# Second mixer of a fused transformer kernel: another order of masks, exponentials, weight splits and norms on three engines

## The reference, cut to what matters

```
h = rms_norm_2(x, attn_norm);  proj = h @ w_in                  # 1024 -> 5444 columns
aq, ak, av, iq, ik, iw, bq, bk, bv, gates = split_cols(proj)
aq, ak, bq, bk = rope(head-wise rms_norm of each); iq = rope(iq); ik = rope(rms_norm(ik))
score = sum_h iw[h] * relu(iq[h] . ik / 8);  keep the 64 best causal keys of each query
ya = softmax(aq . ak / 8 over the kept keys) @ av               # sparse, 8 heads
lam = exp(sum(dl0*dl1)) - exp(sum(dl2*dl3)) + lam_init
yb = (softmax(bq0 . bk0) - lam * softmax(bq1 . bk1)) @ bv       # differential, 4 heads
yb = rms_norm(yb, b_subln) * (1 - lam_init)
x = x + (sigmoid(g_a) * (ya @ w_up_a) + sigmoid(g_b) * (yb @ w_up_b)) @ w_out
```

## Time and profile before

| what | value |
|---|---|
| runs of the kernel before | 1838.51, 1839.82, 1843.36 us; median 1839.82 us |
| the profiled execution | 1841.48 us, its span 1839.8 us |
| PE busy | 1794.3 us, 98% of the span |
| DVE busy | 1122.3 us, 61% |
| ACT busy | 936.7 us, 51% |
| POOL busy | 195.0 us, 11% |
| mean granted TensorE clock | 0.998 of full |
| mixer 2 of layer 0, of layer 1 | tile 0 at 1050.3 us, at 1442.3 us of the span |

### The profile page before, as it was taken

One profiled execution on the slowest core, in us unless ns is written; L12 is line 12 of the kernel. 1 busy time (PEld: TensorE's weight loads), 2 busy tenths in 40 slices (PEclk: granted clock), 3 DMA queues, 4 the chain that ended last, 5 costly groups with the idle time before them and its releaser, 6 DMA issues.

```text
span 1839.8 us, 23640 instructions
## 1 busy us (share of the span) xinstructions
PE 1794.3 (98%) x8740; PEld 1459.0 (79%) x8740; DVE 1122.3 (61%) x1649; ACT 936.7 (51%) x1266; POOL 195.0 (11%) x226
## 2 busy tenths in 40 slices
PE   7999999999999999999999999999999999999999
PEld 6888887788888888877888876778888777788887
DVE  5555676655555555777555489765554688765553
ACT  5444475544454444666444476655444656745441
POOL 0000020000000000200000095100001383000000
PEclk9999999999999999999999999999999999999999
DMA  8556462465556564543555464445555544345551
GB/s 254 184 191 222 139 184 93 151 197 191 196 157 189 190 218 143 181 130 123 186 192 196 160 206 142 156 138 175 187 194 190 203 145 155 130 147 181 186 207 64
DMA packets 221017, 316.21 MB, mean 172 GB/s; under 512 B 14056, under 2 KB 162176, under 8 KB 220672
## 3 DMA queue, kind: packets, MB, share of 16 engines
q1 hardware_dynamic: 220928, 315.03, 52.5%
HBM read 313.94 MB, written 1.05 MB: 171 GB/s over the span
## 4 chain that ended last, share of the span: by engine, by line
PE 81%; DVE 8%; issue 3%; ACT 3%; DVEq 2%; POOL 1%; DMA 1%; SPq 1%; POOLq 0%; ACTq 0%
PE ps L1829 25%; PE ps L1831 24%; PE ps L1830 24%; DVE w_lo L1145 2%; PE ps L1938 2%; ACT w_hi L679 1%; PE ps L1839 1%; PE ps L2034 1%; PE ps L2022 1%; PE ps L2010 1%; PE ps L1973 1%; DVE score L1604 1%; DVE att L1362 1%; DVEq L1607 1%; PE ps L2314 1%
## 5 line engine op out<-in xcount | busy, mean ns | idle before, releaser
L1145 DVE TENSOR_TENSOR w_lo<-raw,w_hi 128x2048 fp32r<-128x2048 f32 (+1 forms) x297 | 671.1, 2281 | 242.3 <-ACT w_hi L679 241.0
L1829 PE MATMUL ps<-w_hi,aT_hi 128*128 128x512 f32 (+2 forms) x1728 | 690.3, 399 | 12.9 <-DVE w_lo L1298 4.8
L1831 PE MATMUL ps<-w_hi,aT_lo 128*128 128x512 f32 (+2 forms) x1728 | 671.3, 388 | 0.0
L1830 PE MATMUL ps<-w_lo,aT_hi 128*128 128x512 f32 (+2 forms) x1728 | 669.4, 387 | 0.0
L679 ACT ACTIVATE w_hi<-raw 128x2048 fp32r<-128x2048 f32 (+1 forms) x297 | 554.7, 1899 | 182.4 <-PE ps L1831 178.8
L1829 PEld LDWEIGHTS ps<-w_hi,aT_hi 128*128 128x128 f32 x1728 | 325.8, 189 | 90.4 <-issue 15.2
L1831 PEld LDWEIGHTS ps<-w_hi,aT_lo 128*128 128x128 f32 x1728 | 325.4, 188 | 68.4
L1830 PEld LDWEIGHTS ps<-w_lo,aT_hi 128*128 128x128 f32 x1728 | 326.4, 189 | 59.6
L729 ACT ACTIVATE att<-ps,rstd 128x256 f32<-128x256 f32 x132 | 55.6, 472 | 377.9 <-PE ps L1831 377.8
L1219 DVE SCALAR_TENSOR_TENSOR att<-ps,rstd,att 128x256 f32<-128x256 f32 x132 | 57.8, 479 | 287.3 <-ACT att L729 287.3
L1829 PE MATMUL ps<-w_hi,gT_hi 128*128 128x512 f32 x528 | 207.1, 392 | 0.0
(11 more groups left out here) (265 smaller groups left out, 1398.0 us busy)
## 6 DMA issues: line engine op xcount, KB each, us to landing
raw<-in_w_in SPq DMA_DIRECT2D x120, 512.0 KB, 4.5
raw<-in_w_ffn_gate SPq DMA_DIRECT2D x88, 512.0 KB, 4.1
raw<-in_w_ffn_up SPq DMA_DIRECT2D x88, 512.0 KB, 5.1
raw<-in_w_ffn_down SPq DMA_DIRECT2D x88, 512.0 KB, 4.4
raw<-in_w_ffn_in SPq DMA_DIRECT2D x88, 512.0 KB, 4.9
raw<-in_w_ffn_out SPq DMA_DIRECT2D x44, 512.0 KB, 4.6
raw<-in_w_out SPq DMA_DIRECT2D x32, 512.0 KB, 4.7
raw<-in_w_ck SPq DMA_DIRECT2D x8, 512.0 KB, 4.2
```

The lines of the kernel that those rows point to most:

```text
L1145: V.tensor_tensor(o, a, h, ALU.subtract).then_inc(units_split, 1)
L1829: M(o, ah, wh, start=start, stop=False)
L1830: M(o, ah, wl, start=False, stop=False)
L1831: return M(o, al, wh, start=False, stop=stop)
```

## The change

Nothing is computed otherwise, except one added operation (below). Instructions trade places in the hand-written queues:

- **ACT, each feed-forward:** one Sqrt of a scratch column after the last `keep`, so that the Sqrt table is loaded there.
- **Start of mixer 2:** ACT splits unit 2 before it stages the second half (layer 0, as layer 1 did), and unit 3 after `evac(0)` in both layers. DVE in layer 1 takes `norm` before unit 3.
- **lam:** ACT's two Exp and DVE's three operations go from behind the first head norm to just ahead of `exps(0)` and `masked(0)`.
- **Turned keys:** `item(0)`, `item(1)`, `item(4)`, `item(5)` go ahead of head squares, sums or roots.
- **DVE:** `masked(0)`, `probs(0)` go ahead of the split of unit 12; `masked(0)` also ahead of one round of `best`; `probs(1)`, `masked(2)`, `masked(3)`, `probs(3)`, `masked(4)`, `probs(4)`, `probs(5)`, `probs(6)` ahead of a split or a gate; `up_a(1, ...)` ahead of the split of unit P2_OUT + 2.
- **ACT:** `exps(1)`, `exps(4)`, `exps(7)` ahead of a split, units 15 and 17 later; the first sigmoid from ahead of `probs_turned(6)` to behind `probs_turned(7)`.
- **PE:** six places at which turned keys or index scores are made are set one or two places later.
- **Mixer 1, DVE:** `probs(10)` ahead of `masked(11)`.

```diff
@@ ACT, ffn
                 keep(FT - 1, FT - 1)
+                act.wait_ge(consts_ready, 1)
+                nc.scalar.drain()
+                nc.scalar.activation(ms[:, 0:1], ident[:, 0:1], ACT.Sqrt)
@@ ACT, mixer 2
                 evac(0)
-                if l == 0:
-                    split(st, 3)
+                split(st, 3)
                 head_squares(0)
                 win_split(2, 0)
                 head_roots(0)
-                act.wait_ge(lam_sums, l + 1)
-                nc.scalar.activation(lam[:, 0:2], lam[:, 0:2], ACT.Exp).then_inc(lam_exp, 1)
                 win_split(2, 1)
...
                 evac(1)
+                item(0)
                 head_squares(1)
                 win_split(3, 1)
                 head_roots(1)
-                item(0)
...
                 win_split(5, 1)
+                item(4)
                 head_roots(3)
-                item(4)
                 win_split(6, 0)
+                act.wait_ge(lam_sums, l + 1)
+                nc.scalar.activation(lam[:, 0:2], lam[:, 0:2], ACT.Exp).then_inc(lam_exp, 1)
                 exps(0)
                 evac(4)
                 win_split(6, 1)
                 probs_turned(0)
+                exps(1)
                 split(st, P2_WIN + 14)
-                exps(1)
...
                 probs_turned(3)
+                exps(4)
                 split(st, P2_WIN + 19)
-                exps(4)
...
                 split(st, P2_UP)
-                act.wait_ge(tile_done, W + 9)
-                gate(GATES2 + DM)
                 probs_turned(6)
+                exps(7)
                 split(st, P2_UP + 1)
-                exps(7)
                 diff_hi()
                 split(st, P2_UP + 2)
                 probs_turned(7)
+                act.wait_ge(tile_done, W + 9)
+                gate(GATES2 + DM)
@@ DVE, mixer 1
+                probs(10)
                 masked(11)
-                probs(10)
@@ DVE, mixer 2
                 win_split(3, 0)
+                item(1)
                 head_sums(1)
                 win_split(3, 1)
                 head_scales(1)
-                item(1)
...
                 head_sums(3)
+                item(5)
                 win_split(5, 1)
                 head_scales(3)
                 best(1)
-                item(5)
-                best(1)
-                win_split(6, 0)
+                dve.wait_ge(lam_exp, l + 1)
+                V.tensor_tensor(lam[:, 2:3], lam[:, 1:2], lam[:, 0:1], ALU.subtract)
+                V.drain()
+                V.tensor_tensor(lam[:, 2:3], lam[:, 2:3], par2[:, 704:705], ALU.subtract)
                 masked(0)
                 best(1)
                 probs(0)
+                win_split(6, 0)
                 win_split(6, 1)
                 masked(1)
                 best(1)
+                probs(1)
                 split(st, P2_WIN + 14)
-                probs(1)
                 head_sums(4)
-                best(1)
-                split(st, P2_WIN + 15)
                 masked(2)
+                head_scales(4)
                 item(7)
-                head_scales(4)
                 best(1)
                 probs(2)
-                split(st, P2_WIN + 16)
+                split(st, P2_WIN + 15)
+                masked(3)
+                best(2)
+                probs(3)
                 best(1)
...
+                masked(4)
                 gate(7, 0)
-                masked(4)
+                probs(4)
                 dve.wait_ge(tile_done, W + 7)
                 gate(7, 1)
+                split(st, P2_WIN + 18)
+                probs_turned(4)
                 split(st, P2_WIN + 19)
-                probs(4)
-                probs_turned(4)
                 masked(5)
...
                 up_b(1)
-                split(st, P2_OUT + 2)
                 up_a(1, 0)
                 up_a(1, 1)
                 stage(B + 6, parts=((0, 1), (1, 1)), first=2, banks=STAGE_BANKS_UP)
+                split(st, P2_OUT + 2)
@@ PE, beside_bk: turn((0, 1)) at 6 -> 8, index_scores(0) at 13 -> 14
@@ PE, beside_aq: index_scores(2) at 1 -> 2, turn((2, 3)) at 6 -> 8
@@ PE, beside_bv: turn((4, 5)) at 9 -> 10, pair_qk(0) at 13 -> 14
```

More of the change, by code:

```diff
@@ L937, in _ @@
                     square_scaled(0)
+                    split(st, 2)
                     stage(B, GAIN_ATTN, PARTS[2:], first=2)
-                    split(st, 2)
                     square(6, 1, junk, 2)
@@ L944, in _ @@
                 else:
-                    turned_in(st, B, GAIN_ATTN + l * KC, l * 2 + 7, P2_WIN)
+                    stage(B, GAIN_ATTN + l * KC, PARTS[:2])
+                    square(l * 2 + 7, 0)
+                    split(st, 2)
+                    stage(B, GAIN_ATTN + l * KC, PARTS[2:], first=2)
+                    square(l * 2 + 7, 1)
+                    squared()
                     root(N)
@@ L1089, in _ @@
                 probs_turned(2)
-                split(st, P2_WIN + 17)
                 exps(3)
@@ L1093, in _ @@
                 item(8)
+                split(st, P2_WIN + 17)
                 split(st, P2_WIN + 18)
                 probs_turned(3)
+                exps(4)
                 split(st, P2_WIN + 19)
-                exps(4)
                 diff_out(3)
@@ L1550, in _ @@
                 else:
-                    turned_in(st, B, GAIN_ATTN + l * KC, P2_WIN)
+                    split(st, 2)
+                    stage(B, GAIN_ATTN + l * KC, PARTS[2:], first=2)
                     norm(N)
+                    split(st, 3)
                 dve.wait_ge(params2_loaded, (l + 1) * 128)
@@ L1702, in _ @@
                 head_scales(0)
-                dve.wait_ge(lam_exp, l + 1)
-                V.tensor_tensor(lam[:, 2:3], lam[:, 1:2], lam[:, 0:1], ALU.subtract)
-                V.drain()
-                V.tensor_tensor(lam[:, 2:3], lam[:, 2:3], par2[:, 704:705], ALU.subtract)
                 win_split(2, 1)
                 win_split(3, 0)
+                item(1)
                 head_sums(1)
@@ L1753, in _ @@
                 V.drain()
-                masked(3)
+                item(9)
+                split(st, P2_WIN + 16)
                 split(st, P2_WIN + 17)
-                item(9)
-                probs(3)
-                split(st, P2_WIN + 18)
                 dve.wait_ge(bias_loaded, (l + 1) * 16)
                 dve.wait_ge(rot_ready, l * 5 + (4 * L + 5))
+                masked(4)
                 gate(7, 0)
-                masked(4)
+                probs(4)
                 dve.wait_ge(tile_done, W + 7)
                 gate(7, 1)
+                split(st, P2_WIN + 18)
+                probs_turned(4)
                 split(st, P2_WIN + 19)
-                probs(4)
-                probs_turned(4)
                 masked(5)
                 gate(8, 0)
+                probs(5)
                 split(st, P2_WIN + 20)
                 gate(8, 1)
-                probs(5)
                 dve.wait_ge(yb_sq, l + 1)
@@ L1777, in _ @@
                 V.tensor_scalar(ms[:, 0:8], ms[:, 0:8], 1.0 / P, EPS, ALU.mult, ALU.add).then_inc(yb_ms, 1)
-                split(st, P2_WIN + 21)
                 probs_turned(5)
                 masked(6)
+                split(st, P2_WIN + 21)
                 dve.wait_ge(yb_root, l + 1)
                 V.reciprocal(ms[:, 0:8], ms[:, 0:8]).then_inc(yb_scale, 1)
+                probs(6)
                 gate(9, 0)
                 split(st, P2_UP)
-                probs(6)
                 sparse_lo(0)
@@ L2361, in beside_bk @@
                 def beside_bk(at):
-                    if at == 6:
+                    if at == 8:
                         rotated(0)
                         turn((0, 1))
-                    if at == 13:
+                    if at == 14:
                         copied(1, 1)
@@ L2369, in beside_aq @@
                 def beside_aq(at):
[L2370 removed]
+                    if at == 2:
                         pe.wait_ge(idx_relu, l * 4 + 2)
                         index_scores(2)
[L2373 removed]
+                    if at == 8:
                         rotated(1)
```

6 lines of the change are left out of this document (2 added, 4 removed).

## The result

The changed kernel takes 1831.45 us (median of 7, 1830.57 to 1832.72), against 1839.82 for the kernel before in the same runs. The ratio is 0.9949, with a 95% interval from 0.9935 to 0.9962: faster by 0.5%. The forecast was 1821.0 with a range of 1814 to 1829, so the sign was right, but the time lies 2.5 us above the range, and of the 18.8 us expected only 8.4 came by the medians. By the ratio the gain is 9.4 us, and by the two profiled executions 1841.5 - 1830.57 = 10.9.

The account below looks back on a forecast made before the run. PE is busy 98% of the span, so only its stalls, mostly in mixer 2, can be won: 2.2 + 4.1 + 2 x 5.1 + 2.3 = 18.8 us off the 1839.8 median gives 1821.0, range 1814 to 1829.

Parts of the forecast that it names:

- The chain that sets R: Mixer 2: DVE's queue to `masked(0)`, then `exps(0)` and `evac(4)` on ACT, set PE's restart, whatever PE wins before.
- The sign that the prediction set for this part: Mixer 2: PE restarts after `evac(4)` near 1114 and 1497, with the wait there still near 2 us each.
- Part one: Mixer 2, from tile 0 to the stall on `evac(4)`: gain of 2.2 us in layer 0 and 4.1 in layer 1.
- the lam term: DVE ahead of `masked(0)`: two lam subtractions put in, 1.2 us at most, about 0.5 without POOL, taken as 0.9.
- Part two: Mixer 2, from PE's restart to the end: `probs` waits and `up_a`'s go, 0.45 comes back; gain 5.1 us a layer.
- Rival 2: Mixer 2: the reorder doesn't bring `probs` forward, as the exponentials' own chain is as long; 1831 us, chance 0.07.
- The clock: Mixer 2, layer 1: the drop behind PE's restart, costing 1.6 us, was left as it is.
- rival 5: Behind PE's restart: a drop in layer 0 too adds 1.6 us, none in layer 1 takes 1.6 off; no separate chance.
- Mixer 1: Turn 10's wait for `probs(10)` goes in both layers: gain 2.3 us.
- Tables: Sqrt load moved from the norms to the feed-forward: hidden in both places, gain 0 and cost 0.
- Rival 1: Mixer 2: DVE and POOL collide more, rotation 0 some 2 us late, half of part two's 9.7 returns; 1828 us, chance 0.16.
- Rival 4: Mixer 2: ACT holds `head_squares(1)` back for rotation 0, standing 5.8 us in layer 1, so `masked(0)` is late; 1849 us, chance 0.04.

Follow-up runs that it names:

- items: Kernel after with `item(0)` and `item(1)` set back behind the roots and scales of round 1: 1825.25 us, ratio 0.9912 to the kernel before.
- `best`: Kernel after with one more round of `best` moved from ahead of `masked(0)` to behind it: 1826.34 us, ratio 0.9933 to the kernel before.
- POOL: Kernel after without POOL's arithmetic in rotation rounds 1 to 3, waits and signals kept: 1817.57 us, one run.
- lam: Kernel after with lam set back behind `head_roots(0)` on ACT and `head_scales(0)` on DVE: 1827.56 us, ratio 0.9925 to the kernel before.

## Why the prediction was wrong, step by step

**The chain that sets R: right.** Every edit that moved `masked(0)` in front of `exps(0)` moved R by the same amount to 0.03 us (items, `best`, POOL, lam in layer 1; lam in layer 0 moved them by 1.9 and 1.6), and moving `evac(4)` out of the chain took the stand away. Whatever PE won in front (the first rotation, 2.5 us) went into the stand, as the text said. But I then wrote that PE would wait there "about as long as before (2.0 to 2.7 us)". The same count gives 5.3 with what was measured: in layer 0 PE reaches the bank 2.23 us sooner and R comes 1.04 later, 2.04 + 2.23 + 1.04 = 5.31; in layer 1 it is 2.03 + 3.28 = 5.31. The sign that the prediction set for this part failed as well: R near 1114 and 1497 was forecast, and 1116.85 and 1504.99 came.

**Part one's size: wrong, and the failed step.** I had put the restart R 2.2 us sooner in layer 0 and 4.1 in layer 1; it came 1.04 later and not sooner at all. The 3.7 us taken out were right. The terms set against them, 0.9 for lam and 0.6 for `item(0)`, were too small, and the longer splits beside POOL stood at nothing. In layer 0 `masked(0)` came 1.04 late instead of 2.2 early, 3.24 us off. Up to the first index score (t0+35.92 before, +37.68 after) the kernel lost 1.76, where I had 0.6. The squares stood 2.91 us behind `item(0)`, and the splits of units 7 and 8 then ran into POOL, 3.17 and 3.21 us. From there on it won 0.72 instead of 2.8: lam took 2.2 us with its drain and not 0.9, and the split of unit 11 took 3.04, where the one of unit 12 in the earlier trace rows had 2.30. Together 2.1. In layer 1 the same parts are 1.97 and 2.14, together the 4.1 that I had forecast as gain. The idle time of 1.29 did go from its place, but DVE's idle time up to `masked(0)` is as long as before: 3.45 us of it now stand ahead of `item(1)`, and the splits of units 7 and 8 behind it take 3.14 and 3.22 where they took 2.38 and 3.09.

The error in the lam term can be read off. I took its highest price, 1.2, from one pair beside POOL as if it were a ceiling. It depends on how much of POOL's instruction is left when DVE comes, up to 1.3 us for each subtraction here, an estimate from the 1.27 of POOL's line 620.

**Part two: right.** I forecast 4.86 - 0.45 = 4.4 from R to `w_out`. Without a clock drop it is 112.56 before and 108.05 to 108.2 in two of the experiments, so 4.4 to 4.5. The turns 2, 3, 4 and 6 don't wait, turn 7 waits 0.6 for `diff_lo`, and `up_a` gave its 0.73. `evac(5)` and `gate(7, 0)` cost nothing. Rival 2 falls: its 1831 is close to the measured 1831.45, but by chance, since the waits that it kept are all gone.

**The clock: a term left as it was.** Layer 0 had no drop behind R and now has one, worth 1.3; layer 1 kept its own, 1.8 against 1.64. I named the drop as rival 5, but only within the range. The stands of 5.3 us had it in both layers, those of 2.0 only in some executions, a stand of 2.83 had none and one of 2.87 had it (both with the items set back), and in the four kernels whose stands in mixer 2 stayed under 1.7 us there was none in mixer 2. So the drop came with every stand of 2.87 us or more in mixer 2, and below that a stand's length alone doesn't decide it.

**Mixer 1: right.** 2.47 for 2.3. **Tables: right,** nothing.

**The rivals.** Rival 1 had the right mechanism and about the right time for the wrong half: I placed the collisions at rotation 0 and in part two, and they fell on units 7, 8 and 11 and on lam. Rival 4 was partly there as well: ACT stood 5.23 us for `item(0)` in layer 1 (5.8 by my count) and the squares of round 1 came 6.4 us later behind t0 than before, but only a part of that reached `masked(0)`. Setting the items back gave 2.69 us at `masked(0)` in layer 0 and 2.26 in layer 1, against ACT's stands of 2.91 and 5.23.

The sum, redone with the measured terms: mixer 1 -2.5, part one +1.0 and 0.0, part two -4.5 a layer, `up_a` -0.7 a layer, clock +1.3 and +0.2, and -0.4 ahead of tile 0: -10.8, against -11.0 in the spans and -8.4 between the medians. The 0.4 is no reading, as t0 of layer 0 runs from 1046.6 to 1049.5 us in profiles of kernels whose code ahead of it is that of the kernel after. The 2.6 us between the last two are the spread of the kernel before, whose executions here run from 1838.5 to 1845.5; its profiled one is 1.7 above the median, the changed kernel's 0.9 below.

## What to carry to other kernels

When an operation on DVE is moved to where GpSimd is at work, don't cost it by its duration at its old place. Look at what GpSimd does at the new place, and count up to one whole GpSimd instruction (1.3 us here) for each moved one, however small it is, and more where GpSimd has a row without a gap (2.3 us once). Ask also which other operations slide onto GpSimd's by the shift. Before work is cut from a queue, ask which operation hands its result on and what stands in front of that: here two lines swapped on ACT and a scalar put back gave 8 us, and the whole reorder of part one nothing. And when a gain is put "into the slack", write down how long the stand behind it becomes, since a longer stand can cost clock as well.

## What the hardware showed that I had not expected

- A DVE subtraction on 128 x 1 elements takes 0.16 us without POOL beside it and 1.06 to 1.14 beside it. A split takes 2.28 or up to 3.2 beside the rotation, and POOL's rotation step 1.27 or up to 3.35. Mostly they alternate, and each lengthens by what is left of the other's instruction; once a split waited out the rest of a row of POOL's small instructions and took 4.43.
- 1.45 us of work moved off the DVE queue brought its end forward by 2.2 to 2.3 us, and POOL's arithmetic of three rounds, which shares no data with most of that queue, held its end back by 5.8 to 5.9 us.
- The same stand of 2.03 to 2.05 us was followed by a clock drop in one execution and not in another, at the same place with the same work; the drop cost 1.64 us.
- Once PE no longer waited for `exps(0)`, a table load of 1.28 us that had been hidden stood on the chain.
